# Gates and output projection of the first block in unsplit float32, and cross attention with its heads interleaved

## What is computed

```python
def mixer_ab(x, ...):                       # first layer only
    z = rms_norm(x, norm) @ w_in            # 1024 -> 2560: gate, recurrent and pooled parts
    xr = causal_dwconv(z_rec, conv_w, conv_b)
    y_a = gelu(z_gate) * rg_lru(xr, ...)    # rg_lru: sigmoid(xr @ w_gx), sigmoid(xr @ w_ga), 8 heads of 128
    y_b = multi_scale_pool(z_pool, ...)     # 4 groups of 128, each @ w_g
    return concat([y_a, y_b]) @ w_out       # 1536 -> 1024
def cross_attn(x, mem, ...):                # layers 0 and 1; 4 heads of 256, 256 memory tokens
    q, k, v = rms_norm(x) @ wq, m @ wk, m @ wv
    p = softmax(q @ k.T * 256 ** -0.5)
    return (p @ v) @ wo
```

## Time and profile before

| | |
|---|---|
| median of 3 runs | 1822.09 us (1818.46 to 1822.68) |
| the profiled execution | 1822.83 us, of it span 1821.0 us |
| TensorE busy in the span | 94% |
| mean granted TensorE clock | 0.957 |

### The profile page before, as it was taken

How to read it: one execution, slowest core, us unless ns; L and a number is a source line. 1 busy time by engine, 2 the same in 40 slices (tenths; PEclk the granted TensorE clock), 3 DMA queues, 4 the chain that set the end, 5 groups by cost and what they waited for, 6 DMA issues and landing times.

```text
span 1821.0 us, 30499 instructions
## 1 busy us (share of the span) xinstructions
PE 1703.2 (94%) x11722; PEld 1373.0 (75%) x11722; DVE 859.4 (47%) x1410; ACT 628.7 (35%) x1067; POOL 487.7 (27%) x269
## 2 busy tenths in 40 slices
PE   8998989999999998999998999988889999989886
PEld 7887989999998797999998998877844443433333
DVE  2787447888863353678884335765411001000002
ACT  2383444344442444444344333654311111111101
POOL 0433423555433132355552443221100000000000
PEclk9999999999999989999997999998889999999997
DMA  7464524555548442455532554332879999999993
GB/s 267 153 209 145 181 90 131 180 178 184 180 145 247 141 161 84 128 183 182 175 128 95 183 184 142 102 105 69 318 309 409 409 409 410 410 409 410 409 409 148
DMA packets 112992, 401.10 MB, mean 220 GB/s; under 512 B 12544, under 2 KB 17024, under 8 KB 112512
## 3 DMA queue, kind: packets, MB, share of 16 engines
q1 hardware_dynamic: 111888, 395.82, 60.2%
q10 hardware_dynamic: 1008, 3.96, 0.6%
HBM read 394.02 MB, written 1.05 MB: 217 GB/s over the span
## 4 chain that ended last, share of the span: by engine, by line
PE 37%; issue 31%; DVE 23%; ACT 7%; POOL 1%; DVEq 1%; DMA 0%; ACTq 0%; SPq 0%; POOLq 0%
DVE wl L1137 6%; DVE cf L1438 5%; PE pw L1848 5%; PE pw L1849 5%; PE pw L1850 5%; ACT wh L652 4%; PE pw L2082 4%; DVE hid L1454 3%; PE acc L1848 3%; PE acc L1850 3%; PE acc L1849 3%; DVE cf L1441 3%; PE acc L1857 2%; PE acc L1968 2%; DVE gpad L1432 1%
## 5 line engine op out<-in xcount | busy, mean ns | idle before, releaser
L1023 POOL TENSOR_TENSOR wl<-raw,wh 128x1024 fp32r<-128x1024 f32 x165 | 403.6, 2447 | 570.2 <-ACT wh L652 569.5
L652 ACT ACTIVATE wh<-raw 128x1024 fp32r<-128x1024 f32 x330 | 341.8, 1051 | 282.4 <-PE pw L1850 161.0
L1848 PE MATMUL pw<-ah,wh 128*128 128x256 f32 x1416 | 410.8, 290 | 4.0 <-DVE gt L1588 4.0
L1849 PE MATMUL pw<-ah,wl 128*128 128x256 f32 x1416 | 406.3, 287 | 0.0
L1850 PE MATMUL pw<-al,wh 128*128 128x256 f32 x1416 | 405.9, 287 | 0.0
L1137 DVE TENSOR_TENSOR wl<-raw,wh 128x1024 fp32r<-128x1024 f32 x165 | 214.2, 1299 | 206.3 <-ACT wh L652 206.2
L1848 PEld LDWEIGHTS pw<-ah,wh 128*128 128x128 f32 x1416 | 277.8, 196 | 8.5 <-issue 7.1
L1849 PEld LDWEIGHTS pw<-ah,wl 128*128 128x128 f32 x1416 | 278.0, 196 | 0.0
L1850 PEld LDWEIGHTS pw<-al,wh 128*128 128x128 f32 x1416 | 277.4, 196 | 0.0
L1848 PE MATMUL acc<-yh,wh 128*128 128x256 f32 x832 | 245.9, 296 | 23.7 <-POOL yl L1092 5.4
L1850 PE MATMUL acc<-yl,wh 128*128 128x256 f32 x832 | 242.0, 291 | 0.0
(11 more groups left out here) (291 smaller groups left out, 2414.1 us busy)
## 6 DMA issues: line engine op xcount, KB each, us to landing
raw<-in_stream SPq DMA_DIRECT2D x502, 512.0 KB, 3.9
ring_w<-in_stream SPq DMA_DIRECT2D x96, 512.0 KB, 14.6
ring_y<-in_stream SPq DMA_DIRECT2D x72, 512.0 KB, 14.6
ring_m<-in_stream SPq DMA_DIRECT2D x48, 512.0 KB, 14.2
ring_h<-in_stream SPq DMA_DIRECT2D x24, 512.0 KB, 14.7
shifted<-hpad SPq DMA_DIRECT2D x16, 177.5 KB, 5.0
mem_t<-in_mem ACTq DMA_DIRECT2D x2, 1024.0 KB, 7.7
shifted<-hpad SPq DMA_DIRECT2D x16, 106.5 KB, 6.3
```

The costliest lines, as they stand in the source:

```text
L652: A.done(act.activation(wh[:, s.base % SPLIT, :], raw[:, slot_of(s.base), :], ACT.Copy), w_hi)
L1023: G.done(pool.tensor_tensor(wl[:, s.base % SPLIT, :], raw[:, slot_of(s.base), :], wh[:, s.base % SPLIT, :].bitcast(F32), ALU.subtract), w_ ...
L1848: pe.matmul(dst, wh[:, s.base % SPLIT, w], hi, start=start, stop=False, **kw)
L1849: pe.matmul(dst, wl[:, s.base % SPLIT, w], hi, start=False, stop=False, **kw)
```

## The change

Two parts. First, the four gate slabs and the twelve slabs of `about` are no longer split: TensorE multiplies them in float32 from `raw` (`tile1`), with the unsplit activations `xr` and `z`. The 16 splits on ACT, 8 on DVE and 8 on POOL, go, and with them all high and low parts of `xr`, the pooled part and the two results, on ACT, DVE and POOL. The slots of `about` come free when TensorE is through with a slab and not when it is split. Because the numbering of splits skips the gate slabs, DVE now splits the first key slab of each pair and POOL the second. Second, the cross attention is written in another order: the scores of heads 0 and 1 stand inside the query phase (after query slabs 4 and 6), the scores go to banks `acc[1]` to `acc[3]`, and each later step of a head has work of another head beside it. In the diff below, the pieces are in this order: which slabs are unsplit; ACT in `gk`; ACT in the query phase of `cross(l)`; DVE in `gk`, in `v0` and in `queries(l)`; TensorE's helpers, gate slabs and `about`.

```diff
 def unsplit(s):
-    return s < S0["gk"] or S0["cw"] <= s < S0["cw"] + CW
+    if S0["gk"] <= s < S0["v0"]:
+        return (s - S0["gk"]) % 3 == 0
+    return s < S0["gk"] or S0["about"] <= s < S0["q0"] or S0["cw"] <= s < S0["cw"] + CW
...
+            act.wait_ge(S("pooled"), 4)
             for n in range(4):
                 split(At(gate_slab(n) + AHEAD))
...
-                wait_emptied(act, USE0["gk"] + 5 * n + 2)
-                A.done(act.activation(yh[:, 8 + n, :], z[:, 16 + n, :], ACT.Copy), S("yb_hi"))
...
+                for n in range(KC):
+                    split(At(S0[f"q{l}"] + n + AHEAD))
+                    for c in range(2 * n - 8, 2 * n - 6) if l == 0 and n >= 4 else ():
+                        mem_hi(1, c)
+                    if n == 6:
+                        x_exp(l, 0)
...
-                dve.wait_ge(S("yb_hi"), n + 1)
-                V.done(dve.tensor_tensor(yl[:, 8 + n, :], z[:, 16 + n, :], yh[:, 8 + n, :].bitcast(F32),
-                                         ALU.subtract), S("yb_lo"))
...
-                if n:
-                    ya_lo(n - 1)
                 if n == 4:
                     v0_out(0)
...
+                    if n == 5:
+                        x_max(l, 0)
+                    if n == 6:
+                        x_scale(l, 0)
+                x_max(l, 1)
+                x_scale(l, 1)
+                x_max(l, 2)
+                x_scale(l, 2)
+                x_low(l, 0)
+                x_max(l, 3)
+                x_scale(l, 3)
+                x_low(l, 1)
+                x_low(l, 2)
+                x_low(l, 3)
...
+            def tile1(dst, s, n, src, start, stop, **kw):
+                return pe.matmul(dst, raw[:, slot_of(s.base), n * P:n * P + P], src, start=start, stop=stop, **kw)
+            def x_score(l, h):
+                wait_emptied(pe, USE0[f"q{l}"] + 2 * h + 1)
+                for qt in range(TT):
+                    r = 2 * h + qt
+                    if r >= 3:
+                        pe.wait_ge(S("cross_scalar"), x_count(X_ACT, l, "exp", (r - 3) // 2, (r - 3) % 2))
+                    for c in range(2):
+                        last = pe.matmul(acc[1 + r % 3][:, 0:T], q_t[:, 2 * h + c, qt * P:qt * P + P],
+                                         k_t[:, 2 * h + c, :], start=(c == 0), stop=(c == 1))
+                    last.then_inc(mm_done, 1)
...
-                wait_split(pe, s)
+                wait_raw(pe, s)
...
-                    pe.wait_ge(S("xr_lo"), h + 1)
+                    pe.wait_ge(S("xr_ready"), h + 1)
                     for g in range(2):
-                        last = tile3(pw[(u + e) % 4][:, g * T:g * T + T], s, 2 * e + g, yh[:, h, :], yl[:, h, :],
-                                     True, True)
+                        last = tile1(pw[(u + e) % 4][:, g * T:g * T + T], s, 2 * e + g, xr[:, h, :], True, True)
...
+            for n in range(12):
+                s = At(S0["about"] + n)
+                wait_raw(pe, s)
+                if n < 4:
+                    wait_emptied(pe, USE0["gk"] + 5 * n + 2)
+                else:
+                    pe.wait_ge(S("ya_ready"), n - 3)
+                for c in range(KC):
+                    last = tile1(acc_of(c), s, c, z[:, 16 + n, :] if n < 4 else xr[:, n - 4, :],
+                                 n == 0 and c % 2 == 0, n == 11, skip_group_check=True)
```

More of the change, by code:

```diff
@@ L96, in _uses, with x_count, x_bank @@
     USES.extend(who)
-def _attn_uses(n):
-    out = []
-    for h in range(n + 1):
-        if h < n:
-            out += ["a", "a"]
-        if h >= 1:
-            out += ["a", "a", "v"]
-    return out
+X_PE = [("score", 0), ("score", 1), ("turn", 0), ("score", 2), ("mix", 0), ("turn", 1), ("score", 3), ("mix", 1),
+        ("turn", 2), ("turn", 3), ("mix", 2), ("mix", 3)]
+X_ACT = [("exp", 0), ("exp", 1), ("exp", 2), ("high", 0), ("exp", 3), ("high", 1), ("high", 2), ("high", 3)]
+X_PARTS = {"score": 2, "turn": 2, "mix": 1, "exp": 2, "high": 1}
+def x_count(order, l, kind=None, h=0, qt=0):
+    total = sum(X_PARTS[k] for k, _ in order)
+    at = order.index((kind, h)) if kind else 0
+    return total * l + sum(X_PARTS[k] for k, _ in order[:at]) + qt + 1
+def x_bank(kind, h):
+    order = [(k, n) for k, n in X_PE if k != "score"]
+    return sum(X_PARTS[k] for k, _ in order[:order.index((kind, h))])
 HEADS2 = [("d", i) for i in range(4)] + [("s", i) for i in range(8)]
@@ L139 @@
 _uses("q0", "v" * 8)
-_uses("x0", _attn_uses(XH))
+_uses("x0", "".join("aa" if k == "turn" else "v" for k, _ in X_PE if k != "score"))
 _uses("f0", "vv" * FJ)
@@ L145 @@
 _uses("q1", "v" * 8)
-_uses("x1", _attn_uses(XH))
+_uses("x1", "".join("aa" if k == "turn" else "v" for k, _ in X_PE if k != "score"))
 _uses("f1", "vv" * FJ)
@@ L553, in _ @@
                 sp.dma_start(x[:, 4 * half:4 * half + 4, :], x_in[:, 4 * half:4 * half + 4, :]).then_inc(x_landed[half], 16)
-            for s in range(3 * RAW):
+            for s in range(6 * RAW):
                 load(At(s))
@@ L563, in shift_out @@
                                      hpad[32 * b:32 * b + 32, lo:hi, turn:turn + n]).then_inc(landed, 16)
-            early, late = S0["cw"] // RAW - 3, -(-(S0["cw"] + CW) // RAW) + 1
+            early, late = S0["cw"] // RAW - 6, -(-(S0["cw"] + CW) // RAW) + 1
             with sp.Fori(0, early) as i:
                 for j in range(RAW):
-                    load(At(3 * RAW + j, RAW, i))
-            for s in range((early + 3) * RAW, late * RAW):
+                    load(At(6 * RAW + j, RAW, i))
+            for s in range((early + 6) * RAW, late * RAW):
                 load(At(s))
@@ L709, in _ @@
                     mem_hi(0, 2 * n - 15)
-                if n in (9, 12, 15, 18):
-                    g = n // 3 - 3
-                    act.wait_ge(S("pooled"), g + 1)
-                    A.done(act.activation(yh[:, 8 + g, :], z[:, 16 + g, :], ACT.Copy), S("pooled_hi"))
                 if n >= 14:
@@ L745, in _ @@
                     split(At(S0["v0"] + n + 1 + AHEAD))
-                act.wait_ge(S("ya_ready"), n + 1)
-                A.done(act.activation(yh[:, n, :], xr[:, n, :], ACT.Copy), S("ya_hi"))
             for n in range(8):
@@ new lines, in x_exp, with x_turned @@
+            def x_exp(l, h):
+                for qt in range(TT):
+                    r = 2 * h + qt
+                    act.wait_ge(S("cross_max"), 2 * XH * l + r + 1)
+                    A.done(act.activation(prob[:, h % 2, qt, :], acc[1 + r % 3][:, 0:T], ACT.Exp,
+                                          bias=nmax[:, qt:qt + 1], accum_out=den[:, qt:qt + 1]), S("cross_scalar"))
+            def x_turned(l, h):
+                for qt in range(TT):
+                    act.wait_ge(mm_done, x_count(X_PE, l, "turn", h, qt))
+                    b = pw[(USE0[f"x{l}"] + x_bank("turn", h) + qt) % 4][:, 0:T]
+                    A.done(act.activation(pt[:, h % 2, :, qt * P:qt * P + P], b.rearrange("p (a q) -> p a q", a=TT),
+                                          ACT.Copy), empty_a)
@@ L811, in _ @@
             act.dma_start(mem1[:], mem_in).then_inc(S("mem_again"), 16)
-            for n in range(KC):
-                split(At(S0["q0"] + n + AHEAD))
-                for c in range(2 * n - 8, 2 * n - 6) if n >= 4 else ():
-                    mem_hi(1, c)
             cross(0)
@@ new lines, in x_turn @@
+            def x_turn(l, h):
+                for qt in range(TT):
+                    u = USE0[f"x{l}"] + x_bank("turn", h) + qt
+                    wait_emptied(pe, u - 4)
+                    pe.wait_ge(S("cross_prob"), 2 * XH * l + 2 * h + qt + 1)
+                    for kt in range(TT):
+                        last = pe.transpose(pw[u % 4][:, kt * P:kt * P + P],
+                                            prob[:, h % 2, qt, kt * P:kt * P + P], ident[:])
+                    last.then_inc(mm_done, 1)
@@ new lines, in x_mix @@
+            def x_mix(l, h):
+                u = USE0[f"x{l}"] + x_bank("mix", h)
+                wait_emptied(pe, u - 4)
+                wait_emptied(pe, USE0[f"x{l}"] + x_bank("turn", h) + 1)
+                for dc in range(2):
+                    for kt in range(TT):
+                        last = pe.matmul(pw[u % 4][:, dc * T:dc * T + T], v_m[:, kt, h_cols(h, dc)],
+                                         pt[:, h % 2, kt, :], start=(kt == 0), stop=(kt == TT - 1))
+                last.then_inc(mm_done, 1)
```

188 lines of the change are left out of this document (71 added, 117 removed).

## The result

The changed kernel's median is 1795.83 us (4 runs, 1793.12 to 1800.93), against 1821.89 for the kernel before on the same chip; the ratio of the means is 0.9864, 95% interval 0.9838 to 0.9890. The profiled execution took 1800.93 us with a span of 1799.1.

A forecast was written before the change was run, and what follows sets the result against it. TensorE, busy 94% of 1821.0 us, was taken as the bound, with its waits to pay for dearer tiles. Terms of -1.7, -3.7 and -10.0 summed to -15.4, giving 1807.0 us after a small allowance; range 1801 to 1814.

The forecast's parts named there:

- The tile's price: Gates and output projection: an unsplit tile takes 0.430 us against 0.362 split, adding 7.9 us over 116 tiles.
- Output projection, -3.7: Last value matmul to last projection matmul: 45.0 us becomes 41.3 as split wait, value-copy wait and low clock go.
- Cost 0: Query slabs behind the projection load one by one and are split later, covered by 11 slabs or 38 us.
- Gates and keys, -1.7: Gates and key slabs: 20 dearer tiles add 1.4 us, 3.1 of 4.1 us of waits go, 1.0 left.
- Cross attention, -5.0 a layer: Both cross attentions: the new order leaves 1.3 of 6.3 us of TensorE waits, -10.0 us in all.
- the walk said 1.3: Cross attention, new order stepped through: three short waits left, of 0.3, 0.3 and 0.7 us.
- Queries and SP at 0: Query phase: later loading on SP and later splits cost nothing; without that cover, queries wait for a load and a split.
- The tail: Late stages streaming the experts' weights: a shift of the early stages passes through one to one.
- The rivals with a chance of their own: Whole kernel: late value copy or gate waits 0.20, no gain 0.06, slower by the clock 0.04, more than forecast 0.06.
- that one (-20): Gates and cross attention: no waits left there, -20 us or so, 1802; chance 0.06.
- the value copy was not late: Rival ahead of the projection: value copy stays late or gates keep their waits, 1810 to 1814 us; chance 0.20.
- the clock stayed at 1.00 in the projection: Rival in the projection: unsplit tiles at 1.2 GHz cost 0.43 us more each, all 96 giving 1848 us; chance 0.04.

The follow-up runs named there:

- run 4: Changed kernel with DVE's copy of the memory's value product moved from behind head 4 to behind head 7 of the recurrence; one time of 1805.42 us.
- Run 5: `gates_unsplit`: changed kernel with only the output projection split again, gates unsplit and cross attention interleaved; 1807.39 us, ratio 0.9915 to the kernel before.
- Run 3: Changed kernel with ACT's split of query slab q0+2 held back until TensorE is through with projection slab 10; one time of 1800.82 us.
- run 8: Changed kernel with the scores of heads 0 and 1 back behind the last query slab, the rest of the interleaving kept; one time of 1803.1 us.
- `first_part`: Kernel before with only the unsplit gates and output projection, cross attention in the old order; 1808.43 us, ratio 0.9937.
- `proj_unsplit`: Changed kernel with only the gates split again, projection unsplit and cross attention interleaved; 1804.35 us, ratio 0.9896 to the kernel before.
- `cross_only`: Kernel before with only the interleaved cross attention, gates and projection still split; 1806.18 us, ratio 0.9929.
- `after_again`: The changed kernel run again unaltered, for a second profile and more times; 1798.50 us, ratio 0.9870 to the kernel before.
- run 7: Changed kernel with the projection's eight slabs of the heads' rows split again, only its four pooled slabs unsplit; 1800.03 us, ratio 0.9888 to the kernel before.

## Why the prediction was right and where it was wrong

- **The tile's price** (0.068 us): right. 0.433 a tile at clock 1.00 in the changed kernel, and 0.072 saved per tile where 64 were split again.
- **Output projection, -3.7:** right for what it spans, the last value matmul to the last one of the projection. That was 45.03 us (149.26 to 194.29) and is 41.60 (143.80 to 185.40), so -3.4. The value copy's wait, POOL's and the low clock went as said, and runs 4 and 5 showed that the first is a matter of what stands ahead of the copy, and that such a wait can carry some 3 us of low clock.
- **The step that failed: the projection's walk stopped at its last matmul, and the query slabs' splits behind it were put at "Cost 0".** The norm sums behind the projection are in no term of the sum. Before the change a query split on DVE, which shares its four buffers with the projection's splits, stood ahead of `x_res` and held them up: 1.27 us of wait, 0.75 by which ACT's squares came later, and 0.70 of low clock. It went with the projection's splits. The prediction said that the query slabs are "split later"; in fact the split that counts was done 23 us ahead of `x_res`. Run 3 shows it. That is 2.7 us in two of three profiles of the changed kernel and 2.3 in the third.
- **Gates and keys, -1.7:** mechanism right, mis-sized: -2.5 to -3.5. The waits came to 0.6, not the 1.0 left for caution, and the stage before the change stood at 36.23 in the second profile (its granted clock in 92:124 was 0.95, and 1.00 in the one of the forecast). The values' 0.56 us, a wait of 0.26 for a POOL split among them, were in no term. Run 5 showed what the forecast did not see: the `yl` it blamed belongs to the projection's edit.
- **Cross attention, -5.0 a layer:** right in kind and nearly in size, -5.7 and -5.6. Waits of 6.3 became 1.1 where the walk said 1.3. The other 0.5 is mostly that a wait costs 0.15 us or more beyond its brackets, which count from the modelled end of the matmul before: the last query matmul pitches at 0.12 and starts at 227.01, so that 227.80 is 0.67 late and not 0.52. There were five such waits, and two are left.
- **Queries and SP at 0:** right within 0.1 us in two profiles; 0.9 more in the third, with the longer low clock. The moved scores cost some 0.3 us there in layer 0: `first_part`, which leaves them out, takes 25.49 at the same clock.
- **The tail:** "I let a shift of the early stages pass through it one to one" held: 1079.4 us before and 1073.5 to 1081.7 after.
- **The rest:** 0.9 us in `f0`..`q1`, by the clock as run 8 shows, and some 1.3 us of mean difference in the untouched head and tail, less than the scatter of either.

So 21.9 us are in stages where the forecast had 15.4: 2.7 for the norm, 1.3 for the gates, 0.6 for the values, 1.3 for two cross attentions, 0.9 for `f0`..`q1`, less 0.3 in the queries. The missed norm term is the largest, but alone it would not have left the range, and the 0.9 that the clock gave in `f0`..`q1` is luck and not in any mechanism of the forecast. All of them bring 1807.0 to about 1800.5; the 4.7 us from there to the median are within the scatter of executions (the same kernel's medians in the experiments were 1798.50 and 1797.46). The rivals with a chance of their own were all on the other side but one, and that one (-20) only took waits away from the places edited; none looked at the stages behind. That is why the range ended at 1801. No rival happened: the value copy was not late, if by little (it ends at 144.01, and TensorE needs it at 144.07), and the clock stayed at 1.00 in the projection.

## What to carry to other kernels

When an edit frees shared buffers, follow the instructions that were waiting for them, on every engine's list, until they are past the next stage's first need; here the largest missed gain was one 1.2 us split that stood ahead of a sum. A wait of some microseconds on TensorE is to be priced with the slower matmuls that can follow it (5.16 us of pause came with 2.8 more in the projection). And a change can pay by making the busiest engine's instructions dearer, if that empties the lists of those that it waits for; whether the cheaper instruction would also do is a separate experiment, and here its 4.6 us in the projection shrank to 1.7 to 2.1 over three stages, and to nothing that the whole shows.

## What the runs showed of the hardware

- Executions of one program differ by 4 to 15 us with the mean granted clock (`proj_unsplit` and `cross_only` are the ends): `after_again` took 1793.32 us at 0.965 and 1802.75 at 0.959, about 1.6 us for 0.001. In 190:200 of two profiles of the changed kernel the granted clock was 0.84 and 0.66, with TensorE busy for 9.81 and 9.91 of 10 us. The stages here repeat within 0.1 us wherever the clock is 1.00, so they tell more of an edit than the whole does.
- A pause does not always bring the clock down: behind 1.88 us it stayed at 1.00 (run 7), behind 5.00 it was 0.50 for 4.8 us (run 4). Behind 3.17 it was 0.85 in one profile of the kernel before, and 1.00 in 152:163 of the other, with the same 3.17; there it was 0.51 in 163.60:170.50, around a wait of 4.5 us for POOL. `gates_unsplit`, with the same 3.17, had 0.99 in 155:165 and 0.67 in 165:175, around its own 4.5.
- And the clock falls without a pause: at 189.7 us in the changed kernel, where TensorE had been busy for 3.80 of the last 3.95 us with the norm sums.
